# A second unit's weight half split into an idle buffer, and a residual addition ahead of a weight split, in a fused two-block transformer kernel

## The reference

```
# first block, layer 0 ("dense"), D_FF = 3584
h = rmsnorm(x, ffn_norm[0])
x = x + (silu(h @ wg) * (h @ wu)) @ wd

# second block, the last step ("ff1"), D_FF_2 = 2816
h = modulate(rmsnorm_2(s, g_pre), shift, scale)
gate, up = split(h @ w_in)
s + 0.5 * mod * rmsnorm_2((silu(gate) * up) @ w_out, g_post)
```

## Time and profile before

| what | us |
|---|---|
| median of 3 timed runs | 2598.52 |
| their range | 2598.46 to 2598.67 |
| the profiled execution, its own time | 2589.69 |
| its span, first to last instruction | 2587.9 |
| busy in it: TensorE matmul | 2498.3 |
| VectorE | 1804.8 |
| ScalarE | 1447.9 |

### The profile page before, as it was taken

The page is one execution under the profiler, slowest core; times in us unless marked ns, Lnnn a source line. Parts: engine busy times, 40 slices in busy tenths (PEclk is TensorE's granted clock), DMA queues, the critical chain, the costliest instruction groups (busy, mean ns, idle before and its releaser), DMA issues.

```text
span 2587.9 us, 32745 instructions
## 1 busy us (share of the span) xinstructions
PE 2498.3 (97%) x11767; PEld 1989.3 (77%) x11767; DVE 1804.8 (70%) x1708; ACT 1447.9 (56%) x1564; POOL 70.9 (3%) x54
## 2 busy tenths in 40 slices
PE   7989999989999999999999999999999999998999
PEld 6668887657888888888888787888884777777787
DVE  6554456558999999989898985655544575777544
ACT  4554344546777777777777775435432343466443
POOL 0000000011000000000000000600000000000000
PEclk9999999989999999999999999999999999999999
DMA  6885552759999999999999996655544344434652
GB/s 217 311 284 195 180 193 82 260 179 360 394 375 371 364 366 368 366 365 362 377 348 380 350 345 216 232 186 186 188 146 124 113 130 139 133 103 163 216 191 68
DMA packets 330910, 642.13 MB, mean 248 GB/s; under 512 B 14440, under 2 KB 113288, under 8 KB 330632
## 3 DMA queue, kind: packets, MB, share of 16 engines
q1 hardware_dynamic: 328088, 631.02, 69.5%
q0 software_dynamic: 2736, 9.96, 1.0%
HBM read 633.07 MB, written 7.86 MB: 248 GB/s over the span
## 4 chain that ended last, share of the span: by engine, by line
PE 87%; DVE 6%; ACT 4%; DMA 1%; issue 1%; POOL 0%; SPq 0%; DVEq 0%; ACTq 0%; POOLq 0%
PE ps L941 21%; PE ps L854 19%; PE ps L981 11%; PE ps L896 9%; PE ps L1361 6%; PE ps L788 5%; PE ps L1390 2%; PE ps L1292 2%; PE ps L1095 1%; DVE Bs L2474 1%; DVE As L2387 1%; PE ps L867 1%; PE ps L966 1%; DVE ringL L2357 1%; PE ps L1348 1%
## 5 line engine op out<-in xcount | busy, mean ns | idle before, releaser
L2387 DVE TENSOR_TENSOR As<-ringA,As 128x2048 fp32r<-128x2048 f32 x318 | 731.6, 2301 | 202.6 <-ACT As L1681 133.0
L941 PE MATMUL ps<-As,xgs 128*128 128x512 f32 x2688 | 646.2, 392 | 5.4 <-DVE As L2387 3.9
L941 PEld LDWEIGHTS ps<-As,xgs 128*128 128x128 f32 x2688 | 499.0, 188 | 112.1 <-issue 5.5
L1764 ACT ACTIVATE As<-ringA 128x2048 fp32r<-128x2048 f32 x224 | 428.8, 1914 | 105.4 <-PE ps L941 101.9
L854 PE MATMUL ps<-As,xs 128*128 128x512 f32 x1456 | 374.4, 395 | 3.9 <-DVE hh L2424 3.9
L981 PE MATMUL ps<-Bs,hds 128*128 128x512 f32 x1332 | 322.5, 391 | 5.7 <-DVE hds L2455 2.5
L854 PEld LDWEIGHTS ps<-As,xs 128*128 128x128 f32 x1456 | 271.9, 189 | 63.0 <-DVE hh L2424 4.8
L981 PEld LDWEIGHTS ps<-Bs,hds 128*128 128x128 f32 x1332 | 248.6, 188 | 62.6 <-issue 9.3
L2474 DVE TENSOR_TENSOR Bs<-ringB,Bs 128x2048 fp32r<-128x2048 f32 x111 | 254.1, 2289 | 20.9 <-ACT Bs L1803 19.7
L1803 ACT ACTIVATE Bs<-ringB 128x2048 fp32r<-128x2048 f32 x111 | 213.1, 1920 | 63.2 <-PE ps L981 62.5
L896 PE MATMUL ps<-Bs,hds 128*128 128x512 f32 x1056 | 248.0, 390 | 0.0
(11 more groups left out here) (416 smaller groups left out, 3218.7 us busy)
## 6 DMA issues: line engine op xcount, KB each, us to landing
ringA<-in_moe_w_gate SPq DMA_DIRECT2D x112, 1024.0 KB, 6.7
ringA<-in_moe_w_up SPq DMA_DIRECT2D x112, 1024.0 KB, 6.6
ringB<-in_moe_w_down SPq DMA_DIRECT2D x112, 1024.0 KB, 6.8
ringA<-in_w_ff_in SPq DMA_DIRECT2D x132, 512.0 KB, 4.7
ringA<-in_w_in SPq DMA_DIRECT2D x56, 1024.0 KB, 5.3
ringA<-in_w_ada SPq DMA_DIRECT2D x36, 1024.0 KB, 5.7
ringB<-in_w_ff_out SPq DMA_DIRECT2D x33, 1024.0 KB, 5.0
ringA<-in_dense_w_gate SPq DMA_DIRECT2D x28, 512.0 KB, 3.7
```

The costliest lines, as they stand in the source:

```text
L941: m = mm(ps[:, bank, :], lhs(l, tt, k), As[:, h, r, k % 4, :], start=k == 0 and n == 0, stop=k == KC - 1 and n == 2)
L1764: A(As[:, h, 0, :, :], ringA[:, (p["a"] + u) % 2, 4 * h:4 * h + 4, :], ACT.Copy).then_inc(A_high, 1)
L2387: V.tensor_tensor(As[:, h, 1, :, :], ringA[:, (p["a"] + u) % 2, 4 * h:4 * h + 4, :], f32(As[:, h, 0, :, :]), ALU.subtract).then_inc(A_spli ...
```

## The change

Two edits.

- In both stages (`early=True`), half 0 of the second unit's gate and up weights is split into `Bs` and not into `As[:, 0]`. ScalarE's copy no longer waits for `A_lo_free`, and TensorE's `gu` reads the weights for these 24 matmuls from `Bs`. ScalarE's copy of the first unit's down weights into `Bs` waits, in return, until TensorE has read the second unit's half 0 (`A_lo_free`, one count further).
- In the dense entry VectorE's order changes: `add_out(p, 1, 0)` and the scaling of tile 0 come ahead of both splits of the first unit's weights, where the first split stood ahead of that addition.

```
--- before.py
+++ after.py
@@ -838,6 +838,7 @@
                                 m.then_inc(A_lo_free, 1)
 
                 def gu(i, u, h):
+                    early = rows and isinstance(i, int) and i == 0 and u == 1 and h == 0
                     a_ = e * (2 * nb) + i * 4 + (2 * (p["q"] + u) + h + 1)
                     for tt in range(T):
                         bank = tt if T == 2 else u
@@ -851,7 +852,8 @@
                                 pe.wait_ge(xsm, ready + h)
                         for k in range(4 * h, 4 * h + 4):
                             for n, (l, r) in enumerate(((0, 0), (0, 1), (1, 0))):
-                                m = mm(ps[:, bank, :], lhs(l, tt, k), As[:, h, r, k % 4, :], start=k == 0 and n == 0, stop=k == KC - 1 and n == 2)
+                                w = Bs[:, k // 2, r, k % 2 * BW:(k % 2 + 1) * BW] if early else As[:, h, r, k % 4, :]
+                                m = mm(ps[:, bank, :], lhs(l, tt, k), w, start=k == 0 and n == 0, stop=k == KC - 1 and n == 2)
                         if h == 1:
                             m.then_inc(tile_done, 2 // T)
                     if h == 0:
@@ -1690,7 +1692,7 @@
                 for h in range(2):
                     A(xs[:, 0, 4 * h:4 * h + 4, :], src[:, 4 * h:4 * h + 4, :], ACT.Copy).then_inc(high, 1)
 
-            def feed(p, T, e=0, ahead=False, head=1, leads=True, drains=True, before=None, within=None, split_rows=None):
+            def feed(p, T, e=0, ahead=False, head=1, leads=True, drains=True, before=None, within=None, split_rows=None, early=False):
                 nb = p["nb"]
 
                 def hidden(i, u):
@@ -1709,7 +1711,11 @@
                     if within and isinstance(i, int):
                         within(2 * i + u)
                     nxt = (i + 1, 0) if u else (i, 1)
-                    if not last or ahead:
+                    lead = early and isinstance(i, int) and i == 0 and u == 0
+                    if lead:
+                        act.wait_ge(A_full[(p["a"] + 1) % 2][0], A_LANDED[p["a"] + 1])
+                        A(Bs[:, :, 0, :], by_rows(ringA[:, (p["a"] + 1) % 2, 0:4, :]), ACT.Copy).then_inc(A_high, 1)
+                    elif not last or ahead:
                         A_parts(p, e, *nxt, 0)
                     if last and split_rows:
                         split_rows(0)
@@ -1734,6 +1740,8 @@
                     v = ffn_count(p, 2, e, i, u, 1, 1)
                     if started(v):
                         act.wait_ge(down_done, v)
+                    if lead:
+                        act.wait_ge(A_lo_free, p["a"] + 2)
                     A(Bs[:, :, 0, :], ringB[:, b0 % 2, :, :], ACT.Copy).then_inc(B_high, 1)
                 blocks(act, nb, body, head)
 
@@ -2017,7 +2025,7 @@
                     rows_high(ffn, 1, hf, col(16 + 8 * l))
                 if l == 0:
                     nc.scalar.preload_act_table(ACT.Silu)
-                    feed(ph["dense"], 2)
+                    feed(ph["dense"], 2, early=True)
             nc.scalar.preload_act_table(ACT.Exp)
             modulation(16, 5)
             act.wait_ge(rt_exp, 1)
@@ -2272,7 +2280,7 @@
             tile_root(1, 2, D, 1e-6)
             split_rows(1)
             nc.scalar.preload_act_table(ACT.Silu)
-            feed(ph["ff1"], 2)
+            feed(ph["ff1"], 2, early=True)
             nc.scalar.preload_act_table(ACT.Sqrt)
             for tt in range(TILES):
                 act.wait_ge(acc_half, tt + 1)
@@ -2391,7 +2399,7 @@
                 for h in range(2):
                     x_low(src, done, h, high, split)
 
-            def feed(p, T, e=0, ahead=False, head=1, leads=True, drains=True, after=None, within=None, split_rows=None, settles=True):
+            def feed(p, T, e=0, ahead=False, head=1, leads=True, drains=True, after=None, within=None, split_rows=None, settles=True, early=False):
                 nb = p["nb"]
 
                 def hidden(i, u):
@@ -2407,7 +2415,10 @@
                     if within and isinstance(i, int):
                         within(2 * i + u)
                     nxt = (i + 1, 0) if u else (i, 1)
-                    if not last or ahead:
+                    if early and isinstance(i, int) and i == 0 and u == 0:
+                        dve.wait_ge(A_high, 2 * (p["q"] + 1) + 1)
+                        V.tensor_tensor(Bs[:, :, 1, :], by_rows(ringA[:, (p["a"] + 1) % 2, 0:4, :]), f32(Bs[:, :, 0, :]), ALU.subtract).then_inc(A_split, 1)
+                    elif not last or ahead:
                         A_parts(p, e, *nxt, 0)
                     if last and split_rows:
                         split_rows(0)
@@ -2787,12 +2798,11 @@
                 if l == 1:
                     dve.wait_ge(mods_ready, 1)
                     chunks(call["ff0c"], dst=hcT, **mod_cols(0, 1))
-                if l == 0:
-                    A_parts(nxt, 0, 0, 0, 0)
                 add_out(p, 1, 0)
                 tile_scale(ffn, 0, x, 1)
                 if l == 0:
-                    A_parts(nxt, 0, 0, 0, 1)
+                    for h in range(2):
+                        A_parts(nxt, 0, 0, 0, h)
                 if l == 0:
                     rows_low(ffn, 0, 0, gain)
                 if l == 1:
@@ -2806,7 +2816,7 @@
                 dve.wait_ge(pj_dve, p["jd"] + 4)
                 dve.sem_inc(x_ready, 1)
                 if l == 0:
-                    feed(ph["dense"], 2, settles=False)
+                    feed(ph["dense"], 2, settles=False, early=True)
 
                     def settle(tt):
                         dve.wait_ge(down_done, ph["dense"]["s"] + 2 * NB1 - 1 + tt)
@@ -3192,7 +3202,7 @@
             tile_scale("ff1", 1, x, 2)
             plain_rows(1)
             split_rows(1)
-            feed(ph["ff1"], 2, settles=False)
+            feed(ph["ff1"], 2, settles=False, early=True)
             for tt in range(TILES):
                 for half in range(2):
                     c = slice(half * BW, (half + 1) * BW)
```

16 lines of the change are left out of this document (9 added, 7 removed).

## The result

| | before | changed | |
|---|---|---|---|
| median of the timed runs | 2598.6 us (4 runs, 2598.46 to 2600.99) | 2585.05 us (4 runs, 2580.92 to 2586.44) | 13.55 us less |
| ratio | | | 0.9948, 95% interval 0.9932 to 0.9964 |
| predicted | | 2589.1 us, 2585.5 to 2595.0 | 9.4 us less |

What follows compares the result with a forecast made beforehand. TensorE, busy 97% of the span, was taken as the bound, so only its idle or slow time could yield gains. 3.1 + 2.1 + 1.86 + 2.3 = 9.4 us off 2598.52 gave 2589.1 us, range 2585.5 to 2595.

Steps and rivals of the forecast that it cites:

- The residual addition ahead of the split: Dense start: adding before VectorE's weight splits starts tile 0's and tile 1's transposes earlier; 3.1 us, lower bound 1.2.
- The wait for As: Dense stage, ahead of the second unit: reading half 0 from Bs removes TensorE's wait; 2.1 us.
- The wait that is added: ScalarE's first down-weight copy waits for Bs in both stages; cost nothing, hidden by 24 matmuls; uncovered 4.2 us per stage.
- the signs that the prediction had named as wrong: TensorE waiting on hidden low part or Bs; low clock within 157 to 186 us; stages from 600 us on microseconds longer.
- In the last stage 2.3: Last stage, second unit: 2.0 us from the removed wait plus 0.3 from the group behind it running faster.
- The clock term: Dense stage, second unit's first 24 matmuls: 5.5 us instead of 7.37 without the wait; 1.86 us, bounds 0 and 1.86.
- rival 1: Clock gives nothing back, as the lower level falls near the dense start anyway; 7.5 us gain, 2591.0; chance 0.25.
- I carry the difference over: Whole kernel: the timed median's 8.8 us above the profiled execution is kept, so 2598.52 less 9.4 gives 2589.1.
- two drops fewer elsewhere: Downward end of the range: clock drops missing elsewhere in the program, 2585.4 us.
- 2, the late release: Bs freed late makes hidden parts or down weights miss 1.2 us of slack; 2590.7 to 2593.1 us; chance 0.10.
- 3, the gain swallowed by the expert stage: Self-paced transfers in the expert stage lose the dense stage's 7 us, leaving 2.3; 2596 us; chance 0.09.
- 4, slower: The changed kernel comes out slower than before; chance 0.02, its text not given here.

Runs made afterwards that it cites:

- the kernel with the split in between: Changed kernel with VectorE's first weight split placed between tile 0's residual addition and its scaling at the dense entry; 2586.92 us, ratio 0.9976 to before.
- that part alone: Kernel before plus only the second unit's half 0 through Bs, in both stages, with VectorE's old order; 2594.22 us, ratio 0.9991.
- before again: Kernel before, unedited, run once more (also called its copy); 2593.29 us over 14 runs, ratio 0.9990 to the other runs of before.
- last stage alone: Kernel before plus only the last stage's second unit half 0 through Bs, with VectorE's old order; 2593.52 us, ratio 0.9990.
- residual addition alone: Kernel before plus only tile 0's residual addition and scaling ahead of both weight splits; second unit stays in As; 2591.43 us, ratio 0.9976.
- the dense stage alone: Kernel before plus both edits in the dense stage only, last stage as before; 2589.92 us, ratio 0.9971.
- the late release: Changed kernel, but ScalarE's copy of the first down weights waits for all of the second unit's gate and up products; 2604.60 us, ratio 1.0040.

## Why the prediction was right and wrong

**The schedule was right, step by step.** All start times of the dense stage came within 0.5 us of the forecast (153.2, 157.0, 162.35, 165.6, 174.75, 186.2 against 153.08, 156.65, 161.95, 165.18, 174.36, 185.81). The last five are 0.35 to 0.42 early alike, behind weights that landed 0.33 earlier in that execution. "The residual addition ahead of the split", 3.1: measured 3.07. That VectorE's queue and not TensorE holds tile 1's addition: shown by the 1.66 us wait, and by the kernel with the split in between, which loses it. The wait for As, 2.1: measured 2.14 with that part alone. The wait that is added costs nothing: 3.4 us of ScalarE's time and no wait of TensorE; with the release a half unit later TensorE waits 4.7 us in each stage. Ahead of the first down products, and in the whole dense start, the changed kernel shows none of the signs that the prediction had named as wrong. One sign did appear: the stages between 600 us and the last one are 2.0 us longer than in the profile of before (a lead of 5.08 became 3.09). It did not point at the edit; by the later runs single executions differ by more than that.

**Mis-sized terms.** In the last stage 2.3 was 2.07: the 0.3 for the group behind the wait was not there. Its 24 matmuls start 5.61 us ahead of the transposes behind them with the wait (2407.04 to 2412.65) and 5.62 without (2401.88 to 2407.50). The clock term, 1.86, measured 1.70, but it was entered as certain from one profile. Of the three profiles besides the first in which the dense wait of 1.97 stands unfilled, two have the slow group (24 matmuls in 7.20 us from start to start, before again and last stage alone) and one has 5.61 (residual addition alone). In the last stage the same wait had a granted clock of 1.00 in the 3.5 us behind it in all four profiles of it.

**Chance or the order of work?** Two readings of the clock term stand open. One is chance alone. The other is that the residual addition's edit already takes the drop away: the three profiles with the slow group, the first of before included, are those with a wait of 3.95 to 4.29 us ahead of tile 0's transposes, and these transposes are slow in each of them (eight in 1.97 us, at a granted clock of 0.50); the one with the full clock (1.00 from 180.6 to 184.1) is the one in which that wait is 0.94. One profile on that side can't decide it. What is not open is that the drop was gone: in the dense start all profiles of the changed kernel and of the dense stage alone have a granted clock of 1.00 on tile 0's transposes (eight in 1.09 or 1.10 us), on the 12 matmuls behind the new wait (3.00) and on the second unit (5.66). So rival 1, that the drop falls near the dense start anyway, did not come there; by the total alone it was close (7.5, with 9.7 measured and 1.6 either way). What spoke for it, the same wait with and without a drop, the later traces show again: 24 matmuls behind 1.97 us took 7.36 and 7.37 us in two more profiles and 5.77 in one. Elsewhere in the program the drops vary from execution to execution as well: 20.7 us between two spans of the same instructions, at mean granted clocks of 0.989 and 0.980.

**The step that failed** is the one that made a time of the sum: "I carry the difference over: 2598.52 - 9.4 = 2589.1". The three runs behind 2598.52 agreed to 0.2 us, and I took that for the width of the measurement, although the profiled execution of the same kernel lay 8.8 us lower and "no row says where these lie". The 8.8 were the warning: single executions spread over 15 us and more, and the distance of the profiled execution from its median is no property of the program. It lay 8.8 us under the median in before, 17.2 above it in the copy of before, and 0.5 under it in the changed kernel. Over 103 runs before has a mean of 2595.7; from there 9.4 less is 2586.3, 1.3 us above the measured median and 0.2 from the mean of all 25 runs of the changed kernel. The range then had the same fault: it allowed "two drops fewer elsewhere" for the changed kernel, and nothing for the draw of before. The excess of 13.55 over 9.7 is that draw: 2.9 us because the first four runs of before were slow, 1.0 because the first four of the changed kernel were fast. The size of the miss is luck of the draw; that the result came to lie at the lower edge is not: the range hung on the same baseline, and of all 25 runs of the changed kernel the median, 2585.3, is just below it and the mean, 2586.1, just inside. Why the first four of before came out so close together and so high stays open: later runs of the same program did not repeat it, and nothing on record tells chance from some condition of that first measurement.

**The other rivals.** 2, the late release: did not come, its margin was as computed (the hidden parts at 184.27, needed at 185.81). 3, the gain swallowed by the expert stage: excluded by the dense stage alone. Its first products do wait for a landing in each execution, and that transfer takes 5.65 to 8.13 us from one profile to the next, which adds to the spread; before (5.95 and 5.65) and changed (6.54, 5.77 and 6.62) don't differ by it in a way that these profiles could tell. 4, slower: excluded by the interval. Drops elsewhere move without an edit, since they differ between executions of one program (a granted clock of 1.00 and 0.90 between 450 and 500 us in before and its copy), and no run here shows how much of them an edit moves.

## What to carry to other kernels

A gain of a few us in a kernel of 2600 is read between two events on either side of the edit, in one profile each; here that gave 9.1 us from a single pair, where single times scatter by 15. Agreement of three runs (0.2 us here) is not their uncertainty: if a profiled execution lies far from the median of the timed ones, widen the range of both kernels, or ask for more runs, before a sum is subtracted. And a split that waits for its buffer can borrow one that is idle until the next step of the pipeline, as long as its release comes early enough for what is written there next: here the 24 matmuls behind it (5.5 us) were cover enough, and without them TensorE waited 4.7 us.

## What the runs showed of the hardware

- The same instructions took spans of 2587.9 and 2608.6 us, at mean granted clocks of 0.989 and 0.980; most of the difference, 15.8 us, is there before the expert stage, in a stretch of 600 us where TensorE is busy for 552.7 and 555.9 us, at a granted clock of 0.97 and 0.94; in the expert stage it is busy for 952.2 to 953.2 of 960 us, at 1.00 in both.
- In windows that lie within a drop the granted clock reads 0.50 (before, 181 to 183 us), outside one 1.00 (184 to 187).
- A wait of 1.97 or 1.98 us was followed by a drop in some executions and not in others: 24 matmuls of 128x512 in 7.2 or in 5.6 us, start to start, at a granted clock of 0.54 to 0.64 or of 1.00 over 3.5 us. It came in three of four profiles in the dense stage and in none of four in the last.
- Every longer wait at these places was followed by a drop to 0.50. Behind 3.92 to 4.29 us ahead of tile 0's transposes eight of these took 1.97 us in five of five profiles; behind 3.83 us ahead of the last stage's first unit 12 matmuls took 4.36 to 5.46 us in twelve of twelve, where the next twelve took 3.0; behind 4.72 and 4.79 us in the late release 24 took 7.94 and 7.83. Behind waits of 0.82 to 2.22 us ahead of tile 0's transposes these took 1.09 or 1.10 in seven of seven.
- Transposes of 128x128 were slower at the lower clock as well: eight of them take 1.97 us at 160.05, at a granted clock of 0.50 (160 to 162), and 1.10 at 156.65 in the changed kernel, at 1.00 (156.65 to 157.75).
